# Expert rows weighted at eviction and added to the residual rows in DRAM by an adding DMA, its landing awaited one block later, token rows turned mid-block

## The reference

```
x = x + differential_attention(rms_norm(x))        # 8 heads, causal, T5 bias
h = rms_norm(x)
g = argmax(softmax(h @ w_group + b_group)); g_p = its probability      # 4 groups
e1, e2 = top 2 of the group's 8 experts; w = softmax(their logits) * g_p
for each of a token's two experts e:
    x[token] += w_e * ((silu(h @ w_gate[e]) * (h @ w_up[e])) @ w_down[e])   # 1024 -> 512 -> 1024
out = rms_norm(x)
```

## Time and profile before

| | |
|---|---|
| median of 3 runs | 2765.66 us (2765.53 to 2765.75) |
| the profiled execution, its own time | 2767.84 us |
| its span, first to last instruction | 2766.3 us |
| mean granted TensorE clock | 0.914 |
| busy: PE, PEld, DVE, ACT, POOL | 2358.6, 1888.7, 1421.0, 1187.6, 667.5 us |
| DMA | 473.63 MB, 171 GB/s over the span |

### The profile page before, as it was taken

One profiled execution on the slowest core, in us unless ns is written; L12 is line 12 of the kernel. 1 busy time (PEld: TensorE's weight loads), 2 busy tenths in 40 slices (PEclk: granted clock), 3 DMA queues, 4 the chain that ended last, 5 costly groups with the idle time before them and its releaser, 6 DMA issues. The chain is left out here.

```text
span 2766.3 us, 36992 instructions
## 1 busy us (share of the span) xinstructions
PE 2358.6 (85%) x11480; PEld 1888.7 (68%) x11480; DVE 1421.0 (51%) x2813; ACT 1187.6 (43%) x1605; POOL 667.5 (24%) x464
## 2 busy tenths in 40 slices
PE   4999999964999999999959996577999999999920
PEld 3888889962666666666647885466888887887720
DVE  6121211003667666666535665555656565666646
ACT  5111111111666666766632221445555455555523
POOL 0000000001676666666500111100111011111133
PEclk7999999985999999999979997798999999999965
DMA  4333332134344544443145441567876786786758
GB/s 160 122 116 122 126 114 83 46 99 107 94 118 128 128 129 108 129 128 87 40 151 183 124 119 54 212 255 283 308 270 228 279 296 236 268 311 258 293 226 313
DMA packets 228007, 473.63 MB, mean 171 GB/s; under 512 B 20073, under 2 KB 72465, under 8 KB 225874
## 3 DMA queue, kind: packets, MB, share of 16 engines
q1 hardware_dynamic: 202738, 388.92, 41.5%
q0 software_dynamic: 17072, 53.79, 5.8%
q10 hardware_dynamic: 8112, 29.89, 3.2%
HBM read 355.32 MB, written 117.21 MB: 171 GB/s over the span
## 5 line engine op out<-in xcount | busy, mean ns | idle before, releaser
L650 PE MATMUL ps_s<-k_st,q_st 128*128 128x512 f32 (+3 forms) x1280 | 413.6, 449 | 41.3 <-DVE top L574 29.4
L1319 DVE TENSOR_TENSOR gu_lo<-gu_raw,gu_hi 128x2048 fp32r<-128x2048 f32 x128 | 293.3, 2292 | 160.7 <-ACT gu_hi L1250 118.0
L571 DVE TENSOR_SCALAR_CACHE_REDUCE p_ring<-ps_s 128x256 f32<-128x256 f32 (+7 forms) x352 | 277.7, 792 | 167.4 <-PE ps_s L650 162.2
L650 PEld LDWEIGHTS ps_s<-k_st,q_st 128*128 128x128 f32 x1280 | 242.1, 202 | 175.8 <-issue 90.4
L523 ACT ACTIVATE p_ring<-p_ring,shift 128x1152 f32<-128x1152 f32 (+15 forms) x256 | 305.9, 1197 | 70.6 <-DVE shift L587 70.6
L494 POOL TENSOR_TENSOR p_ring<-p_ring 128x1152 f32<-128x1152 f32 (+15 forms) x128 | 321.6, 2513 | 10.7
L1250 ACT ACTIVATE gu_hi<-gu_raw 128x2048 fp32r<-128x2048 f32 x128 | 239.0, 1909 | 178.8 <-DMA gu_raw<-in_moe_w_up 103.3
L685 PE MATMUL ps_o<-aT,v_st 128*128 128x512 f32 (+3 forms) x640 | 292.2, 540 | 0.0
L512 ACT ACTIVATE aT<-ps_t 128x512 f32<-128x512 f32 (+1 forms) x320 | 168.2, 532 | 227.0 <-PE ps_t L670 226.9
L1411 PE MATMUL ps_g<-gu_hi,xT_lo 128*128 128x512 f32 x720 | 237.1, 411 | 4.3 <-DVE xT_lo L1334 3.6
L1411 PE MATMUL ps_g<-gu_lo,xT_hi 128*128 128x512 f32 x720 | 231.5, 403 | 0.0
(11 more groups left out here) (221 smaller groups left out, 3951.3 us busy)
## 6 DMA issues: line engine op xcount, KB each, us to landing
gu_raw<-in_moe_w_gate SPq DMA_DIRECT2D x128, 512.0 KB, 8.7
gu_raw<-in_moe_w_up SPq DMA_DIRECT2D x128, 512.0 KB, 10.1
d_raw<-in_moe_w_down SPq DMA_DIRECT2D x64, 1024.0 KB, 5.0
qk<-stage SPq DMA_DIRECT2D x64, 512.0 KB, 2.7
q_st<-qk SPq DMA_DIRECT2D x128, 256.0 KB, 5.0
y_rows<-y_sb ACTq DMA_DIRECT2D x45, 512.0 KB, 3.5
y_rows<-nil SPq DMA_DIRECT2D x32, 512.0 KB, 6.0
w_raw<-in_diff_w_in POOLq DMA_DIRECT2D x12, 1024.0 KB, 6.6
```

What stands on the lines that cost most here:

```text
L571: ins = nc.vector.tensor_scalar(p(r, k0, k0 + far), ps_s[:, c % 2, 0:far], SCALE, None, ALU.mult, ALU.max, accum_out=top[:, r % 4, m, col: ...
L650: mm = pe.matmul(ps_s[:, c % 2, j:j + e], q_st[:, g % 2, hl, m, a * P:(a + 1) * P], k_st[:, h % 2, m, k0 + j:k0 + j + e], start=hl == 1, s ...
L1319: nc.vector.tensor_tensor(gu_lo[:, j * GC:(j + 1) * GC], gu_raw[:, j], gu_hi[:, j * GC:(j + 1) * GC].bitcast(F32), ALU.subtract).then_inc( ...
```

## The change

The scratch tensor `y`, the zeros written to it, the kept logits and the gathers in `finish` go. `mix_and_route` now works out each token's two weights in its pipeline: `choose` makes differences of logits, ACT takes their Exp at the end of its step (for tile n-5), and `place` waits for it and makes the weights, so that each entry of `slots` holds a token and a weight. Entries that nobody fills point to 128 dump rows behind the last token, with weight 0; SP clears the dump rows at the start of `attend`. In `run_experts`, ACT's eviction multiplies with the weight of the row, and POOL adds the rows to the rows of `x2` in DRAM with an indirect adding DMA. It loads the second copy of the list (`to_rows`) only when the add before has landed, which it awaits a block later, behind the gather for a later block. PE turns the next block's rows in the middle of `gate_up`. `finish` loads all 16 tiles at once into 16 buffers, norms and stores them.

```diff
+            for dump in (scratch["h2"], scratch["x2"]):
+                sp.dma_start(dump[SEQ:SEQ + P].rearrange("p (k d) -> p k d", k=4),
+                             nil[:, :].unsqueeze(1).to_broadcast([P, 4, D // 4])).then_inc(nil_out, 16)
...
-                if n >= 0 and n % 9 == 5 and cleared < BLOCKS_MAX - EXPERTS:
-                    sp.dma_start(spare[cleared].rearrange("p (k d) -> p k d", k=4),
-                                 nil[:, :].unsqueeze(1).to_broadcast([P, 4, D // 4])).then_inc(nil_out, 16)
-                    cleared += 1
...
+            pool.wait_ge(empty_set, 1)
+            pool.dma_start(scratch["slots"].rearrange("(p n) o -> p (n o)", p=P),
+                           empty[:, :, :].rearrange("p n o -> p (n o)")).then_inc(zeroed, 16)
...
-                                                tok[:, q:q + 1], None).then_inc(scattered, 16)
+                                                tokw[:, q, k, :], None).then_inc(scattered, 16)
...
                     act.wait_ge(routed, t + ROUTED0)
                     nc.scalar.activation(h2T[:, :], ps_c[:, :], ACT.Copy).then_inc(h2T_set, 1)
+                if has(at, 5):
+                    q = 1 - par
+                    act.wait_ge(chosen, (n - 5) * 13 + 13)
+                    nc.scalar.activation(e5[:, q, :], x5[:, q, :], ACT.Exp).then_inc(exped, 1)
...
-                link = chain(chosen, t * 14)
+                link = chain(chosen, t * 13)
...
+                nc.vector.tensor_scalar(x5[:, q, 0:GROUPS_E], lg[:, 0:GROUPS_E], gm[:, 0:1], None, ALU.subtract)
+                nc.vector.tensor_tensor(x5[:, q, 4:5], ev[:, 1:2], ev[:, 0:1], ALU.subtract)
...
-                nc.vector.tensor_copy(kept[:, bass.ds(t, 1), 0:4].rearrange("p o n -> p (o n)"), lg[:, 0:4])
-                nc.vector.tensor_copy(kept[:, bass.ds(t, 1), 4:6].rearrange("p o n -> p (o n)"), ev[:, 0:2])
-                link(nc.vector.tensor_copy(e_all[:, bass.ds(t, 1), :].rearrange("p o n -> p (o n)"), eid[:, q, :]))
                 nc.vector.tensor_tensor(both[:, q, :], own[:, q, 0, :], own[:, q, 1, :], ALU.add).then_inc(both_set, 1)
...
-                link = chain(placed, t * 6)
+                link = chain(placed, t * 9)
...
-                nc.vector.tensor_copy(rank_all[:, bass.ds(t, 1), :].rearrange("p o n -> p (o n)"), rank[:, q, :])
...
+                gate(dve, exped, t + 1, passed)
+                link(nc.vector.tensor_reduce(e_sum[:, :], e5[:, q, 0:GROUPS_E], AX.X, ALU.add))
+                link(nc.vector.scalar_tensor_tensor(out=den[:, :], in0=e5[:, q, 4:5], scalar=1.0, in1=e_sum[:, :],
+                                                    op0=ALU.add, op1=ALU.mult))
                 dve.wait_ge(freed, t + (FREED0 - 1))
-                link(nc.vector.tensor_copy(tok[:, q:q + 1], tok_f[:, 0:1]))
+                weight = tokw[:, q, :, 1].bitcast(F32)
+                link(nc.vector.reciprocal(weight[:, 0:1], den[:, :]))
+                link(nc.vector.tensor_tensor(weight[:, 1:2], weight[:, 0:1], e5[:, q, 4:5], ALU.mult))
+                nc.vector.tensor_copy(tokw[:, q, :, 0], tok_f[:, 0:1].to_broadcast([P, 2]))
                 link(nc.vector.tensor_tensor(before[:, :], before[:, :], both[:, q, :], ALU.add))
                 nc.vector.tensor_copy(slot[:, q, :], slot_f[:, :]).then_inc(slot_set, 1)
...
+            blocks_of(pool)
+            most = look(pool, 0, COL_MOST, EXPERTS - 2, BLOCKS_MAX - 3)
+            def load_x(b):
                 at = look(pool, b, COL_LIST, 0, SLOTS - P)
                 gate(pool, x_turned, b + X_TURNED0, passed)
...
                 gate(pool, listed_in, b * 16 + 16, passed)
                 pool.indirect_dma_start(xg[:, :], None, scratch["h2"],
                                         bass.IndirectOffsetOnAxis(ap=listed[:, 0:1], axis=0)).then_inc(x_in, 16)
+            def load_rows(k):
+                at = look(pool, k - 1, COL_LIST, 0, SLOTS - P)
+                pool.dma_start(to_rows[:, :], scratch["slots"][bass.ds(at, P), :]).then_inc(rows_in, 16)
+            def add_y(k):
+                gate(pool, y_taken, k + Y_TAKEN0, passed)
+                pool.indirect_dma_start(scratch["x2"], bass.IndirectOffsetOnAxis(ap=to_rows[:, 0:1], axis=0),
+                                        y_sb[:, :], None, compute_op=ALU.add).then_inc(y_out, 16)
+            load_x(0)
+            load_x(1)
+            load_x(2)
+            load_x(3)
+            load_rows(1)
+            add_y(1)
+            with pool.Fori(1, most) as b:
+                load_x(b + 3)
+                gate(pool, y_out, b * 16, passed)
+                load_rows(b + 1)
+                add_y(b + 1)
+            for k in range(2):
+                gate(pool, y_out, most * 16 + k * 16, passed)
+                load_rows(most + (k + 1))
+                add_y(most + (k + 1))
+            gate(pool, y_out, most * 16 + 32, passed)
...
-                act.wait_ge(y_out, k * 16 + (Y_OUT0 - 16))
-                nc.scalar.activation(y_sb[:, :], ps_y[:, :], ACT.Copy).then_inc(y_taken, 1)
-            def store_y(k):
-                gate(act, y_taken, k + Y_TAKEN0, passed)
-                act.dma_start(scratch["y"].rearrange("(b p) d -> b p d", p=P)[bass.ds(k - 1, 1)].rearrange("o p d -> (o p) d"),
-                              y_sb[:, :]).then_inc(y_out, 16)
...
-                if not first:
-                    store_y(b)
...
+            def gate_up(b, ahead=None):
                 pe.wait_ge(x_lo_set, b + 1)
                 for c in range(KC):
+                    if c == KC // 2 and ahead is not None:
+                        turn_x(ahead)
                     if c % GC == 0:
                         pe.wait_ge(gu_ready, b * GS + (c // GC + 1))
...
-                gate_up(b)
-                turn_x(b + 1)
+                gate_up(b, b + 1)
                 down(b)
...
+            for t in range(TILES):
+                sp.dma_start(acc[:, t, :], x2_rows[t]).then_inc(x_in[GROUPS[t]], 16)
+                if t == 0:
+                    sp.dma_start(g_row[:, :], io["norm_final"].rearrange("(o d) -> o d", o=1).to_broadcast([P, D])).then_inc(g_in, 16)
+            for t in range(TILES):
                 gate(sp, done, t + 1, passed)
-                sp.dma_start(out_rows[bass.ds(t, 1)].rearrange("o p d -> (o p) d"), acc[:, i, :]).then_inc(stored[i], 16)
...
+                sp.dma_start(out_rows[t], acc[:, t, :]).then_inc(stored, 16)
+            sp.wait_ge(stored, 16 * TILES)
...
-            with pool.Fori(0, TILES // RING) as q:
-                for i in range(RING):
-                    gate(pool, added, q * RING + (i + 1), passed)
-                    pool.tensor_copy(rows[:, i, :], dest[:, bass.ds(q * (2 * RING) + 2 * i, 2)]).then_inc(rows_set, 1)
-                    gate(pool, rows_set, q * RING + (i + 1), passed)
-                    for k in range(2):
-                        pool.indirect_dma_start(y[:, i, k, :], None, scratch["y"],
-                                                bass.IndirectOffsetOnAxis(ap=rows[:, i, k:k + 1], axis=0)).then_inc(y_in[i], 16)
...
-                for i in range(RING):
-                    act.wait_ge(added, q * RING + (i + 1 + ADDED0))
-                    act.wait_ge(squared, q * RING + (i + SQUARED0))
-                    nc.scalar.activation(sq[:, :], acc[:, i, :], ACT.Square, accum_out=ss[:, i:i + 1]).then_inc(squared, 1)
-                    act.wait_ge(squared, q * RING + (i + 1 + SQUARED0))
-                    nc.scalar.activation(rt[:, i:i + 1], ss[:, i:i + 1], ACT.Sqrt, bias=eps[:, 0:1],
-                                         scale=1.0 / D).then_inc(rooted, 1)
+            for t in range(TILES):
+                act.wait_ge(x_in[GROUPS[t]], 16 * GROUPS.count(GROUPS[t]))
+                if t:
+                    act.wait_ge(squared, t)
+                nc.scalar.activation(sq[:, :], acc[:, t, :], ACT.Square, accum_out=ss[:, t:t + 1]).then_inc(squared, 1)
+                act.wait_ge(squared, t + 1)
+                nc.scalar.activation(rt[:, t:t + 1], ss[:, t:t + 1], ACT.Sqrt, bias=eps[:, 0:1], scale=1.0 / D).then_inc(rooted, 1)
...
+            for t in range(TILES):
+                dve.wait_ge(rooted, t + 1)
+                nc.vector.reciprocal(ri[:, t:t + 1], rt[:, t:t + 1]).then_inc(inverted, 1)
+                dve.wait_ge(inverted, t + 1)
+                nc.vector.scalar_tensor_tensor(out=acc[:, t, :], in0=acc[:, t, :], scalar=ri[:, t:t + 1], in1=g_row[:, :],
                                                op0=ALU.mult, op1=ALU.mult).then_inc(done, 1)
...
-            with dve.Fori(0, TILES // RING) as q:
-                for i in range(RING):
-                    dve.wait_ge(x_in[i], q * 16 + 16)
-                    dve.wait_ge(y_in[i], q * 32 + 32)
-                    a = acc[:, i, :]
-                    nc.vector.scalar_tensor_tensor(out=a, in0=y[:, i, 0, :], scalar=w_all[:, 0, bass.ds(q * RING + i, 1)],
```

(41 more changed lines are left out.)

129 lines of the change are left out of this document (28 added, 101 removed).

## The result

The changed kernel took 2837.1 us (median of 4 runs, 2829.28 to 2841.96) against 2765.6 before: ratio 1.0262, 95% interval 1.0233 to 1.0291. It is slower, as forecast, but by 71.5 us where 26 were forecast, and just inside the upper end of the range.

A forecast was written before the change was run, and what follows sets the result against it. PE was taken to bound the router and expert stages, DMA the last. Router +74, expert blocks +4, their end +4 and last stage -56 gave +26 on 2766.3, less 0.7: 2791.6 us; 8-in-10 range 2772 to 2838.

The forecast's parts named there:

- The router's chain: Router steps: table load, Exp and tail of `place` delay `oT_lo`, `x` and the projection by 5.5 us, in 11 steps.
- The clock term: Router steps: the longer PE gap loses some clock, taken as 0.3 us a step, between 0 and 1.0.
- its last steps: Router's last steps: `x` and the next `choose` come later behind load, Exp and `place`, 10 us in all (8 to 13).
- The covered wait: Rival, router: Exp ends before `oT_hi`, so the router loses only some 3 us; 2721 us, chance 0.10.
- Expert blocks: Expert stage: later Silu, waits for rows and extra DMA work cost +4 us in all (-10 to +45).
- Up to 1.3 more in the few blocks that wait for weights: Expert blocks: extra DMA work, 0.5 MB a block at 414 GB/s, may delay weights by up to 1.3 us.
- I take 0 for most: Expert blocks: `take_y`'s wait for `to_rows` costs most new-weight blocks nothing; 4 us with both landings at their maximum.
- two chains side by side: Expert blocks: rows land 20.0 us from the turn; add to add takes 7.2 + L, free up to L = 14.3.
- The late lists: Rival, expert blocks: late lists in half, 2 us each, 2836 us; chance 0.17 together with the adding DMA binding blocks.
- The end of the experts: Last expert block: the add is issued later than the store was and must land, +4 us (2 to 8).
- The last stage: Last stage: loads 21.5 us, stores 23.4, plus start and end, 49.5 us instead of 105.3; -56 (-49 to -61).
- No drain at a table load: Router: each load counted as 1.28 us; the rival with 1.38 of drain added gave +19, 2811 us, chance 0.08.

The follow-up runs named there:

- exp_early: Changed kernel with Exp moved in ACT's router step from behind h2T to ahead of the wait for the turn of o: 2758.9 us.
- rows_plain_twice: Changed kernel with rows loaded one block ahead and the adding DMA replaced by two plain scatters, the second into another tensor: 2805.9 us.

## Why the forecast came out as it did

- *The router's chain* was right step by step: the load and Exp on it, 11 steps, T + 10.28 against 10.09, 32 table loads against "some 30". *The clock term failed by size*: 0.3 a step was taken between bounds of 0 and 1.0, and it was about 1.2. I read the earlier trace rows as "a longer gap by itself took nothing", and looked only at the gap right ahead of the projection, which did stay short (1.34 us). The wait that `place`, now behind Exp, puts ahead of the ranking, 4.07 us, was not in the sum. In it the clock fell to 1.2 GHz, and it stayed there over 1.1 us of ranking, 1.34 idle and most of the first 16 matmuls. In the gap of the earlier trace rows it was still 1.00 over the first half and 0.90 over the second, and was lost only later. Besides, two of the ten steps before ran at full clock from the start and were only 15.7 us long, and none does now. Router +81 instead of +74, its last steps +11 for +10.
- *The covered wait*, the rival on the other side, is what exp_early builds: with Exp covered the router stage is as long as before. The kernel took 2758.9 us all the same and not the rival's 2721, because the expert blocks and their end cost 46 more in that trace and not 8.
- *Expert blocks: the step that failed.* +4 forecast, +34 measured, in two terms. "Up to 1.3 more in the few blocks that wait for weights" took only the bytes of a write at 414 GB/s. An add takes 2.3 times the engine time of a plain write, most of it falls on the first 3 us of the down loads, and those head a ring that sets the block: 2.3 us in each of eight, 18.6 in all, of which 15.6 go when the adding is left out. And "I take 0 for most" rested on two chains side by side, 20.0 us from the turn and 7.2 + L from add to add; on POOL they are one ring of 17 to 20 us: the eviction waited 145.8 us for rows where no long wait was forecast, and with the rows loaded ahead the ordinary blocks are 7.6 us shorter in all. The landing itself was right (L = 9, measured 8.2), and the turn of the tokens in mid-block, thought a possible help, makes no difference.
- *The late lists*, given 2836 as a rival, were part of this, but held six blocks by 1.0 to 1.4 us and one by 3.9, and not half of them by 2.
- *The end of the experts*: +4 forecast, +10 measured. The add's landing (6.3 us) was inside the bounds; POOL's drain of 6.7 us behind it was not in the sum.
- *The last stage* was right: 45.3 us at a DMA share of 0.97 for 49.5; loads and stores overlap at 382 GB/s over all instead of 414 and 358 with ends added.
- *No drain at a table load*: it was right to go by the trace.
- That 2837.1 lies inside the range is in part luck: the range reached up to 2838 for late lists in half of the blocks, and the late lists were the smaller part of what came.

Trace against trace the miss is 41.7 us (a span of 2834.0 for 2792.3): 7 in the router, 30 in the blocks, 6 at their end and 2.5 in the stages ahead, less 4 in the last stage.

## What to carry to other kernels

When an instruction is put on an in-order engine, follow what stands behind it on every queue and add up the whole ring, across engines, to its own start; two chains that share one queue are one ring, not two with slack. Here a DMA that adds took 2.3 times the engine time of a plain write; it cost the long blocks 2 us each while the weight loads set them, and five blocks 1.2 us each once they didn't. So first ask whether such stretches need to be bound: a queue that waited for the wrong buffer first cost the kernel before 59 us. With Exp covered, rows kept in SBUF and that order mended, the change is worth 32 us against the kernel before with the same order (2674.0 and 2706.4), and 92 against the kernel before as it was. By the traces the last stage is 56 us shorter for it, the blocks 12 longer and their end 7.

## What the hardware showed that I had not expected

- An adding scatter of 128 rows of 4 KB took 2.99 us of all 16 DMA engines against 1.31 plainly, and landed in 8.2 us against 5.1. Issued 4.8 us ahead of a down load, only 28 of its 128 row packets had started when the load was issued, where the plain one was through.
- POOL's queue drained for 6.7 us at the end of the expert stage, after its last indirect DMA had landed and while no DMA packet moved. It was 6.714 us in each of the seven kernels that add and load the rows a second time, 3.162 in the two that shift them in SBUF and wait on POOL, 5.9 and 2.2 with plain writes in their place, 0.8 in rows_plain_twice, and 10.6 in the kernel before, where nothing waited for it. So it goes with the program and not with the run; what sets its length stays open.
- The clock fell to 1.2 GHz while PE was idle for 4.07 us, and 1.06 us of small matmuls in the 2.4 us behind that did not bring it back: 16 matmuls then took 6.7 us. Behind 3.75 us of idle time right ahead of them 16 matmuls took 5.3 us, and in the same place of the changed kernel 5.5.
